# Two feed-forwards of a one-core float32 kernel: eight block products against seven (Strassen), with the weight sums on GpSimd

## The reference, cut to what matters

```python
def swiglu(x, w_gu, w_down):
    gu = x @ w_gu
    g, u = jnp.split(gu, 2, axis=-1)
    return (jax.nn.silu(g) * u) @ w_down

def second_block(x, mem, g_ffn1, w_ffn1_gu, w_ffn1_down, ...):
    x = x + 0.5 * swiglu(rms_norm(x, g_ffn1[layer]), w_ffn1_gu[layer], w_ffn1_down[layer])
    ...
    x = x + 0.5 * swiglu(rms_norm(x, g_ffn2[layer]), w_ffn2_gu[layer], w_ffn2_down[layer])
```

## Time and profile before

| | us |
|---|---|
| median of 3 runs | 1786.37 |
| lowest and highest run | 1785.3 and 1786.94 |
| span of the profiled execution | 1785.4 |

### The profile page before, as it was taken

The page is one execution under the profiler, slowest core; times in us unless marked ns, Lnnn a source line. Parts: engine busy times, 40 slices in busy tenths (PEclk is TensorE's granted clock), DMA queues, the critical chain, the costliest instruction groups (busy, mean ns, idle before and its releaser), DMA issues.

```text
span 1785.4 us, 25187 instructions
## 1 busy us (share of the span) xinstructions
PE 1776.4 (99%) x9274; PEld 1437.2 (80%) x9274; DVE 1062.3 (59%) x2106; ACT 750.5 (42%) x1386; POOL 407.3 (23%) x248
## 2 busy tenths in 40 slices
PE   9999999999999999999999999999999999999998
PEld 7767778776777888888888878879888888888887
DVE  5888777588877665445433445555756654555333
ACT  6464654446454533223222455545444322232222
POOL 4544553455354310000000232220200200000000
PEclk9999999999999999999999999999999999999999
DMA  5422222322212343333333422323321333333332
GB/s 188 125 81 70 60 59 85 97 81 83 67 53 60 96 138 102 95 94 94 106 106 104 150 60 83 95 72 107 95 73 55 92 101 94 94 94 101 99 106 94
DMA packets 49765, 165.53 MB, mean 93 GB/s; under 512 B 5640, under 2 KB 6152, under 8 KB 49672
## 3 DMA queue, kind: packets, MB, share of 16 engines
q1 hardware_dynamic: 48376, 161.47, 30.2%
q10 hardware_dynamic: 1296, 2.84, 0.4%
HBM read 162.12 MB, written 2.17 MB: 92 GB/s over the span
## 4 chain that ended last, share of the span: by engine, by line
PE 97%; DVE 1%; ACT 1%; issue 0%; POOL 0%; DVEq 0%; POOLq 0%
PE proj L1013 78%; PE turned L1302 2%; PE o L1326 2%; PE score L1276 2%; PE turned L1530 1%; PE proj L1460 1%; PE o L1556 1%; PE score L1521 1%; PE proj L1453 1%; PE score L1285 1%; PE o L1652 1%; PE turned L979 1%; PE score L1641 1%; PE score L1163 0%; PE proj L991 0%; PE turned L998 0%
## 5 line engine op out<-in xcount | busy, mean ns | idle before, releaser
L1013 PE MATMUL proj<-hhi,whi 128*128 128x512 f32 x1456 | 580.2, 399 | 0.6 <-DVE tanh L2285 0.3
L1013 PE MATMUL proj<-hhi,wlo 128*128 128x512 f32 x1456 | 568.1, 390 | 0.0
L1013 PE MATMUL proj<-hlo,whi 128*128 128x512 f32 x1456 | 567.3, 390 | 0.0
L1736 ACT ACTIVATE whi<-ring 128x1024 fp32r<-128x1024 f32 x279 | 295.2, 1058 | 622.7 <-PE proj L1013 614.4
L2201 DVE TENSOR_TENSOR wlo<-ring,whi 128x1024 fp32r<-128x1024 f32 x199 | 243.1, 1222 | 164.8 <-ACT whi L1736 164.5
L1013 PEld LDWEIGHTS proj<-hhi,whi 128*128 128x128 f32 x1456 | 274.3, 188 | 59.4 <-issue 6.6
L1013 PEld LDWEIGHTS proj<-hhi,wlo 128*128 128x128 f32 x1456 | 273.4, 188 | 58.8
L1013 PEld LDWEIGHTS proj<-hlo,whi 128*128 128x128 f32 x1456 | 274.0, 188 | 52.8
L759 POOL TENSOR_TENSOR wlo<-ring,whi 128x1024 fp32r<-128x1024 f32 x80 | 194.7, 2435 | 372.6 <-ACT whi L1736 372.0
L771 POOL TENSOR_TENSOR prob<-prob 128x512 f32<-128x512 f32 x36 | 56.6, 1574 | 873.9 <-ACT prob L1732 873.9
L1762 ACT ACTIVATE prob<-prob,negmax 128x256 f32<-128x256 f32 (+3 forms) x208 | 114.4, 552 | 65.5 <-DVE negmax L2274 64.1
(11 more groups left out here) (334 smaller groups left out, 2426.1 us busy)
## 6 DMA issues: line engine op xcount, KB each, us to landing
ring<-wstream SPq DMA_DIRECT2D x287, 512.0 KB, 3.6
arena<-lines SPq DMA_DIRECT2D x28, 256.0 KB, 5.5
arena<-x ACTq DMA_DIRECT2D x4, 512.0 KB, 5.9
out<-arena SPq DMA_DIRECT2D x8, 256.0 KB, 2.9
arena<-mem SPq DMA_DIRECT2D x1, 1024.0 KB, 9.4
ring<-wstream ACTq DMA_DIRECT2D x2, 256.0 KB, 7.3
arena<-hot SPq DMA_DIRECT2D x2, 80.0 KB
par<-params ACTq DMA_DIRECT2D x2, 74.0 KB, 1.9
```

Source lines behind the costliest of these rows:

```text
L1013: mm = pe.matmul(b, rounded(w), rounded(rhs(v, k)), start=(first and n == 0 and p == 0), stop=(last and n == len(blocks) - 1 and p == 2))
L1736: act.activation(rounded(dst), src, ACT.Copy, scale=scale).then_inc(ready, 1)
```

## The change

Each feed-forward keeps four chunk pairs (g and u of chunks 0, 4, 1 and 5) as they are, 8 jobs. The rest becomes 30 fast jobs (`FFN_FAST`). An up job takes the g and the u slot of one chunk, a down job a third of the hidden chunks for two output chunks. It views its weights as 2 x 2 blocks A (output by half of the input) and the activations as 2 x 2 blocks B (half of the input by half of the tokens, TS = 256 columns), and forms four sums of weights and four of activations, seven products in place of eight, and their sums (the Winograd form of Strassen's scheme). A product is 4 blocks (3 in the last third) by three matmuls of 256 columns.

- GpSimd (`weight_sums`): for each job the four weight sums S1 = A21 + A22, A11 - A21 (in the ring, in place), S2 = S1 - A11, S4 = A12 - S2, and the low part of the whole second slot. It makes these for job J+1 while job J runs. Ahead of the first job it makes the activation sums of the normalised input (`operand_sums`, four of 1024 elements and two low parts). The additions of squares now follow the weight sums.
- ScalarE (`weights_high`): high parts of the two slots, of S1 and S2 together, and of S4; it copies the bank contents between the products of an up job into `c1`, `c7` and `c2`; tanh in two halves; one high part of seven operand blocks (1792 elements) for each pair of hidden chunks.
- VectorE: low parts of the first slot in two halves (`a_low`), of S1 and S2 (`s12_low`, which waits for S4), of S4 (`s4_low`); the sums over banks and the gate in halves of 256 columns; the sums of hidden halves (`inner_sums`) and their low part (`inner_low`); in the down part additions of bank halves to the residual.
- TensorE: products in the order 1, 7, 3 of the job before, 6, 4, 2, 5. Three of them add into one bank (R0) with a read of the bank by another engine in between.
- SP: the second slot of a pair is loaded ahead of the first; eight bias rows come in the last four jobs of the first feed-forward and eight after it (before: nine ahead of it, seven after).
- Some semaphores are merged into others, since the change needs more of them; the chunk order of the next norm changes with it, and the final transposes read from other banks.

```diff
+FFN_STD = 4
+FFN_JOBS = 2 * FFN_STD
+FFN_UP = (0, 4, 1, 5, 2, 6, 3, 7, 8, 12, 9, 13, 10, 14, 11, 15, 16, 19, 17, 20, 18, 21)
+FFN_FAST = [("up", c) for c in FFN_UP[FFN_STD:9]] + [("down", 0, m) for m in range(KC // 2)] \
+    + [("up", c) for c in FFN_UP[9:17]] + [("down", 1, m) for m in range(KC // 2)] \
+    + [("up", c) for c in FFN_UP[17:]] + [("down", 2, m) for m in range(KC // 2)]
+FASTS = len(FFN_FAST)
...
+    load2(n0, n0 + FFN_JOBS)
+    for J in range(FASTS):
+        n = n0 + FFN_JOBS + 2 * J
+        load2(n + 1, n + 2)
+        load2(n, n + 1)
...
+    def weight_sums(J):
+        G, q, n, half = g0 + J, J % 2, n0 + FFN_JOBS + 2 * J, fast_half(FFN_FAST[J])
+        a11, a12, a21, a22 = (ring_part(n + i, part, half) for i in range(2) for part in range(2))
+        pool.wait_ge(wload[(n + 1) % RING], 16 * ((n + 1) // RING + 1))
+        if J >= 2:
+            product_done(pool, 5, f, J - 2)
+        pool.tensor_tensor(s_part(SX, q, 0, half), a21, a22, ALU.add).then_inc(sums_ready, 1)
+        pool.wait_ge(wload[n % RING], 16 * (n // RING + 1))
+        pool.wait_ge(sums_ready, 4 * G + 1)
+        pool.tensor_tensor(a21, a11, a21, ALU.subtract).then_inc(sums_ready, 1)
+        pool.tensor_tensor(s_part(SX, q, 1, half), s_part(SX, q, 0, half), a11, ALU.subtract).then_inc(sums_ready, 1)
+        pool.wait_ge(w_hi, 4 * G + U_HI)
+        both = slice(0, 2 * half * P)
+        pool.tensor_tensor(rounded(wlo[:, (n + 1) % RING, both]), ring[:, (n + 1) % RING, both], hi_u[q][:, both],
+                           ALU.subtract).then_inc(u_lo, 1)
+        if J >= 2:
+            product_done(pool, 3, f, J - 2)
+        pool.wait_ge(sums_ready, 4 * G + 3)
+        pool.tensor_tensor(s_part(SX, q, 2, half), a12, s_part(SX, q, 1, half), ALU.subtract).then_inc(sums_ready, 1)
...
+    def fast(J, to, o, w_hi, w_lo, start, ks):
+        for n, k in enumerate(ks):
+            cols = slice(k * P, (k + 1) * P)
+            hi, lo = operand(J, o, k)
+            for p, (w, v) in enumerate(((w_hi, hi), (w_hi, lo), (w_lo, hi))):
+                mm = pe.matmul(to, rounded(w[:, cols]), rounded(v), start=(start and n == 0 and p == 0), stop=False,
+                               skip_group_check=True)
+        return mm
...
+    def p1(J):
+        G = g0 + J
+        pe.wait_ge(w_lo, 4 * G + A11_LO)
+        operands_there(J, B11)
+        if J >= 2:
+            r0_read(pe, R0_LAST, f, J - 2)
+        fast(J, R0[J % 2], B11, *g_parts(J, 0), True, blocks(J)).then_inc(fast_done, 1)
...
+    for J in range(FASTS):
+        if J == LAST_UP + 1:
+            p3(J - 1)
+        p1(J)
+        p7(J)
+        if 0 < J != LAST_UP + 1:
+            p3(J - 1)
+        p6(J)
+        p4(J)
+        if J == FASTS - 1:
+            p5(J)
+            p2(J)
+        else:
+            p2(J)
+            p5(J)
+    p3(FASTS - 1)
+ffn(0, FFN1_JOB, FFN1_AT, N_FIRST, R_FIRST)
...
+    def weights_high(J, what):
+        G, q, n, half = g0 + J, J % 2, n0 + FFN_JOBS + 2 * J, fast_half(FFN_FAST[J])
+        both = slice(0, 2 * half * P)
+        if what == "g":
+            act.wait_ge(wload[n % RING], 16 * (n // RING + 1))
+            if J >= 2:
+                product_done(act, 2, f, J - 2)
+            if J == 1:
+                act.wait_ge(job_done, j0 + FFN_JOBS)
+            high(ring[:, n % RING, both], hi_g[q][:, both], w_hi)
+        if what == "u":
...
+                product_done(act, 4, f, J - 2)
+            high(ring[:, (n + 1) % RING, both], hi_u[q][:, both], w_hi)
+        if what == "s12":
+            act.wait_ge(sums_ready, 4 * G + 3)
+            if J >= 2:
...
+    for J in range(FASTS + 1):
+        G, q, job = g0 + J, J % 2, FFN_FAST[J] if J < FASTS else ("end",)
+        before = FFN_FAST[J - 1] if J else ("start",)
+        if before[0] == "up":
+            act.wait_ge(r1_out, G)
+            act.activation(tanh[:, 1 - q, 0:TS], gsum[:, 1 - q, :], ACT.Tanh, scale=0.5).then_inc(tanh_ready, 1)
+        if job[0] == "up":
+            product_done(act, 1, f, J)
+            if G >= 2:
+                act.wait_ge(r1_out, G - 1)
+            act.activation(c1[:, q, :], R0[q], ACT.Copy).then_inc(r0_out[q], 1)
+        if J < FASTS:
+            weights_high(J, "s4")
+        if before[0] == "down" and before[1] == 2 and J < FASTS:
+            finish_high(before, 0)
+        if job[0] == "up":
+            product_done(act, 7, f, J)
+            if J >= 2:
+                r0_read(act, R0_U4, f, J - 2)
+            act.activation(c7[:, q, :], R2[q], ACT.Copy).then_inc(r2_p7_out, 1)
+        if J + 1 < FASTS:
+            weights_high(J + 1, "g")
+        if before[0] == "up":
+            product_done(act, 3, f, J - 1)
+            act.activation(tanh[:, 1 - q, TS:S], R0[1 - q], ACT.Tanh, scale=0.5).then_inc(tanh_ready, 1)
+        if job[0] == "up":
+            product_done(act, 6, f, J)
+            if G >= 2:
+                act.wait_ge(r2_out, G - 1)
+            act.activation(c2[:, q, :], R0[q], ACT.Copy).then_inc(r0_out[q], 1)
+        if J + 1 < FASTS:
+            weights_high(J + 1, "u")
...
+    def a_low(J, part):
+        G, q, n, half = g0 + J, J % 2, n0 + FFN_JOBS + 2 * J, fast_half(FFN_FAST[J])
+        cols = slice(part * half * P, (part + 1) * half * P)
+        dve.wait_ge(w_hi, 4 * G + G_HI)
+        dve.wait_ge(sums_ready, 4 * G + 3 + part)
+        dve.tensor_tensor(rounded(wlo[:, n % RING, cols]), ring[:, n % RING, cols], hi_g[q][:, cols], ALU.subtract)\
+            .then_inc(w_lo, 1)
...
+    def s12_low(J):
+        G, q, half = g0 + J, J % 2, fast_half(FFN_FAST[J])
+        dve.wait_ge(w_hi, 4 * G + S12_HI)
+        dve.wait_ge(sums_ready, 4 * G + 4)
+        dve.tensor_tensor(rounded(s_pair(SX_lo, q, half)), s_pair(SX, q, half), s_pair(HS, q, half), ALU.subtract)\
+            .then_inc(w_lo, 1)
...
+    def inner_sums(pair):
+        done = 3 * (d0 + pair)
+        dve.wait_ge(inner_done, f * FC + 2 * pair + 2)
+        dve.tensor_tensor(raw[:, T1:T3 + 1:2, :], raw[:, B12::-(B12 - B22), :][:, 0:2, :], raw[:, B11:B12 + 1, :], ALU.subtract)\
+            .then_inc(d_sum, 1)
+        dve.wait_ge(d_sum, done + 1)
+        dve.tensor_tensor(raw[:, T2, :], raw[:, T3, :], raw[:, B11, :], ALU.add).then_inc(d_sum, 1)
+        dve.wait_ge(d_sum, done + 2)
+        dve.tensor_tensor(raw[:, T4, :], raw[:, B21, :], raw[:, T2, :], ALU.subtract).then_inc(d_sum, 1)
...
+    def inner_low(pair, kk):
+        dve.wait_ge(d_hi, d0 + pair + 1)
+        dve.tensor_tensor(rounded(DL[:, kk, :]), raw[:, 0:7, :].rearrange("p a n -> p (a n)"), DH[:, kk, :], ALU.subtract)\
+            .then_inc(d_lo, 1)
...
+    def inner(J, before, tanhs, gates):
+        G, q = g0 + J, J % 2
+        dve.wait_ge(tanh_ready, tanhs)
+        dve.scalar_tensor_tensor(tanh[:, 1 - q, TS:S], tanh[:, 1 - q, TS:S], 1.0, R0[1 - q], ALU.add, ALU.mult)\
+            .then_inc(r0_out[1 - q], 1)
+        r0_read(dve, R0_LAST, f, J - 1)
+        dve.wait_ge(ffn_step, gates)
+        dve.wait_ge(r2_out, G)
+        dve.tensor_tensor(inner_at(before[1]), tanh[:, 1 - q, :], tmp[:, 1 - q, :], ALU.mult).then_inc(inner_done, 1)
+        if pair_of(before) is not None:
+            inner_sums(pair_of(before))
...
+        if before[0] == "up":
+            product_done(dve, 5, f, J - 1)
+            dve.wait_ge(r2_p7_out, G)
+            dve.tensor_tensor(tmp[:, 1 - q, TS:S], c7[:, 1 - q, :], R0[1 - q], ALU.add).then_inc(r0_out[1 - q], 1)
+            product_done(dve, 4, f, J - 1)
+            r0_read(dve, R0_U2, f, J - 1)
+            dve.tensor_tensor(tmp[:, 1 - q, 0:TS], c2[:, 1 - q, :], R2[1 - q], ALU.add).then_inc(r2_out, 1)
+            dve.wait_ge(tanh_ready, tanhs - 1)
+            dve.scalar_tensor_tensor(tanh[:, 1 - q, 0:TS], tanh[:, 1 - q, 0:TS], 1.0, gsum[:, 1 - q, :], ALU.add, ALU.mult)\
...
+        if J == LAST_UP + 1:
+            inner(J, before, tanhs, gates)
+            a_low(J, 1)
+            s4_low(J)
+            inner_low(pair_of(before), d_place(before[1])[0])
+        if job[0] == "down":
+            product_done(dve, 1, f, J)
+            x_add(2 * job[2], 0, R0[q], r0_out[q])
+        if J < FASTS and J != LAST_UP + 1:
+            a_low(J, 1)
+            s4_low(J)
+        if job[0] == "down":
+            product_done(dve, 7, f, J)
+            x_add(2 * job[2] + 1, 1, R2[q], r2_p7_out)
+        if before[0] == "up" and J != LAST_UP + 1:
+            inner(J, before, tanhs, gates)
...
+        if J + 1 < FASTS:
+            a_low(J + 1, 0)
...
+        if J + 1 < FASTS:
+            s12_low(J + 1)
+        if J == 0:
+            inner_low(1, 1)
+        if before[0] == "down" and before[1] == 2:
+            last_of(before, 1)
+        if pair_of(before) is not None and J != LAST_UP + 1:
...
+        if job[0] == "up":
+            product_done(dve, 2, f, J)
+            r0_read(dve, R0_P1, f, J)
+            dve.tensor_tensor(gsum[:, q, :], c1[:, q, :], R1[q], ALU.add).then_inc(r1_out, 1)
...
```

662 lines of the change are left out of this document (452 added, 210 removed).

## The result

The changed kernel takes 1972.56 us (median of four runs, 1969.58 to 1973.84), the kernel before 1785.84 us: a ratio of 1.104, 95% interval 1.1024 to 1.1055. The forecast was 1852 us, at most 1910. The direction was right; of the 186.7 us lost, it had 66.

The account below looks back on a forecast made before the run. VectorE and GpSimd taking turns on SBUF, with a dependency loop through four engines, would bound up jobs; per feed-forward 43.5 + 4 + 18 x 12.5 + 8 x 10.4 + 34 + 2 = 391.7 us, giving 1852 us, range 1792 to 1910.

Parts of the forecast that it names:

- TensorE's floor: Matmul time of one feed-forward: 192 long matmuls, 43.5 us, plus 2436 short ones, 292.3 us, together 335.8 us.
- front part: Four plain chunk pairs opening each feed-forward: 43.5 us of matmuls plus 4 us (1 to 8) for held VectorE work.
- 14 up jobs between others of their kind: Fast up jobs: 12.5 us each, between 11.86 (turns alone) and 13.2 us.
- the first up job and the one ahead of each down phase, with the changes: Up jobs at 12.5 us each, plus 2 us (0 to 3) for changes between up and down jobs.
- The removed columns: TensorE's matmuls: short ones cost 0.120 us each, so the removal saves 23.2 us per feed-forward.
- The mechanism: VectorE and GpSimd take turns for whole SBUF-only instructions; PSUM-operand ones aren't held; 11.86 us of turns per up job.
- The rival that the doors don't bind: VectorE's and GpSimd's SBUF instructions find gaps, TensorE stays unbroken: 1742 us, chance 0.11.
- The loop with GpSimd first: Up-job dependency loop with GpSimd's first sum taking its turn before VectorE's low part: 11.4 and 14.5, mean 12.9 us.
- The loop through the evacuations: Up-job loop through GpSimd's last sum, VectorE's low part and evacuations to the next third product: 11.1 us on average.
- 11.86: Sum of VectorE's and GpSimd's SBUF turns in one up job, in us, against 10.08 that TensorE needs.
- a falling clock: Sign against the forecast: TensorE's granted clock falling in the gaps would make it wrong; no time given.
- everything waits: Rival: GpSimd first each time and longer product waits; up job 13.8, down job 11 us; 1926 us, chance 0.09.

Follow-up runs that it names:

- e2: Changed kernel with GpSimd's weight sums and second-slot low part replaced by write-only memsets of about the same length (values left out): 1897.43 us.
- e14: Changed kernel with the four weight sums on VectorE, the second slot's low part still on GpSimd, last pair's conversion earlier at up-to-down changes: 1946.61 us.
- e15: As e14, but the second slot's low part on VectorE too, so GpSimd has no step in the fast jobs: 1898.95 us.
- e11: Changed kernel with the last pair's conversion (`inner_high`, `inner_low`) moved earlier where up jobs give way to down jobs: 1959.43 us.
- e13: Changed kernel with GpSimd's weight sums, second-slot low part and operand sums as single memsets, and the last pair's conversion earlier at the changes: 1791.7 us.
- e12: Changed kernel with GpSimd's six operand sums in the front part replaced by memsets that read nothing (values left out): 1955.58 us.
- e8: Changed kernel with VectorE's three evacuations of an up job moved ahead of `s12_low` in its queue: 1983.25 us, single run.
- e10: Changed kernel with `a_low` of the next job moved ahead of the finished pair's `inner_sums` on VectorE's queue: 1999.44 us, single run.
- e3: Changed kernel with each GpSimd weight sum and the second-slot low part replaced by one short memset (values left out): 1814.29 us, single run.
- e1: Changed kernel with GpSimd's weight sums and second-slot low part moved to VectorE, and ScalarE's `inner_high` of the last up job earlier: 1916.41 us.

## Why the prediction was wrong in size

The steps of the sum against the trace, for one feed-forward (mean of the two, read off the start of each job's first matmul):

| step | forecast, us | measured, us |
|---|---|---|
| TensorE's floor | 335.8 | 335.8 |
| front part | 47.5 | 60.9 |
| 14 up jobs between others of their kind | 14 x 12.5 = 175 | 14 x 13.34 = 186.8 |
| the first up job and the one ahead of each down phase, with the changes | 4 x 12.5 + 2 = 52 | 81.4 |
| 8 down jobs | 83.2 | 85.5 |
| last phase | 34 | 38.5 |
| sum | 391.7 | 453.1 |

**The step that failed** is the price of the places where the pipeline fills or changes its kind of work. The sum gave 2 us to the changes and no extra to the first fast job (measured 29.4 more than forecast), and 4 us to the front part (13.4 more): 42.8 of the 61.4 us. The up job was 0.84 us too short 14 times, 11.8 us. The lower clock stood in the sum at nothing; the runs don't separate its share.

**Right.** The removed columns: matmuls of 256 columns stand 0.120 us apart, and a down job without a gap takes exactly 10.08 us. By the formula for an isolated warm matmul in the Trainium skill, TensorE: Matmul & The Clock Gate, section "Back-to-back issue gap", an estimate would be 84 x 0.1092 = 9.2 us; the measurement decides. The mechanism: VectorE and GpSimd take turns on SBUF, operations with a PSUM operand don't (406 to 426 ns in all 96 records above), and an up job isn't bounded by TensorE. e2 shows the turns to be worth 75.1 us, e14 against e15 shows one of them nearly alone. The rival that the doors don't bind is out. The Trainium skill, SBUF — State Buffer, section "Who interferes with whom", has issue order decide who blocks; the rows at 887.63 (2.85 us, behind VectorE's of 887.53) and 888.26 (2.51 us, behind GpSimd's of 887.63) above agree.

**The changes between up and down jobs and the first fast job: 52 forecast, 81.4 measured.** This is the largest error, 29 of 61 us, and the one term that was given and not worked out: "2 us, from 0 to 3". At each change the first down product needs the last pair: a serial chain over four engines, tanh, gate, product, three sums, high part, low part of 1792 elements. It is 10 us of idle TensorE at the last change and 5.7 to 7.5 at the others, where the low part also stood behind `s12_low` (e11 gave 13.1 us back by order alone). The last up job takes 25.6 us, the ones ahead of the first two down phases 18.8 and 19.0.

The first fast job takes 18.1 us. Ahead of its sixth product TensorE waits 5.4 and 6.9 us for ScalarE's copy of the bank (0.37 us). ScalarE could have made it when the first product ended, at 693.5. But ahead of it in ScalarE's queue stands the high part of the second hidden pair, which waits for the last of VectorE's `inner_sums`, issued at 699.02:

```profile
699.49 1.70 ACT L2006 ACTIVATE DH<-raw 128x1792 fp32r<-128x1792 f32 x1 [9.46 <-DVE raw L3021]
701.09 0.37 ACT L2359 ACTIVATE c<-score 128x256 f32<-128x256 f32 x1
701.60 0.55 PE L1584 MATMUL score<-TH,HS 128*128 128x256 f32 x1 [5.43 <-ACT c L2359]
```

The order is the same in e13, where this wait is 3.9 us; no run changes it. Even in e13 the four jobs take 60.1 us; 40.3 would be their floor.

**The front part: 4 us added in the forecast, 17.4 measured.** I had counted at most three held jobs. e12 shows 10.5 us of the 17.4 to be GpSimd's operand sums; 4.7 us stay in e13, where GpSimd is light throughout.

**The up job: 12.5 in the forecast, 13.34 measured.** The loop with GpSimd first was 12.9 in my working, and I had chosen below it. That the lengths alternate was right (about 14.7 us, then 12.2 to 13.7), but not where the gaps stand. The forecast had them ahead of the third product. In the 28 steady jobs those sum to 28 us, and the gaps ahead of the first product to 39: there TensorE waits for `a_low`, which stands behind the held `inner_sums`, a path that the working didn't have. Two runs correct the picture further. The loop through the evacuations isn't the only one: e8 cut it and gained nothing, since the gap moved to the first product, and e10 did the reverse. And turns and loop are not alternatives of which the longer counts, as my 11.86 and 12.9 were set against each other: they add up. The working's loop without turns was 11.1 us, e2 without them took 11.75; its turns on top were 1.8 us, the runs show 1.6. Of the 3.26 us over TensorE's floor, GpSimd's length alone makes about half (e3 to e2: 10.17 to 11.75 us on average over both feed-forwards) and its reads the rest (11.75 to 13.34).

**The clock.** The prediction named a falling clock as something that would make it wrong, and left it out of the sum. It fell after the gaps, and the longer products sum to 19.3 us in a feed-forward, a bound for what it cost and no price.

**The rivals.** The time came out beyond "everything waits" (1926 us, chance 0.09), whose up job of 13.8 us was near and whose 3 us for changes was as wrong as mine. The range was too narrow on that side.

**Where 186.7 us went**, as the runs take it apart in steps (each step's share depends on their order): 75.1 us by GpSimd's reads in the weight sums (changed kernel to e2), 83.1 by the length of its work (e2 to e3), 22.6 by the operand sums and the late conversion (e3 to e13; singly 17.0 and 13.1), and 5.9 left (e13 to before). In that last step TensorE's saving, 23.2 us in each feed-forward, meets what e13 loses over TensorE's floor: 4.7 us in the front part, 19.8 in the first fast job and at the changes, 3.8 in the last phase, 0.9 in the steady up jobs, 29.2 in all; 5.0 of these are longer products at the lower clock. (The kernel before stood 2.5 us over its own floor of 359.1, and the difference is smaller by as much.)

**Open.** Why the fast jobs gave 4 us back in e12 I can't say. How much of the half-clock time would have been waited anyway wasn't separated from the gaps either. What the copy ahead of the hidden pair's high part would give back in the first fast job is untested too. And e1's steady job of 11.9 us, with VectorE busy for nine tenths of it, I explain by its in-order queue, without a run that shows it.
